# A fused two-block transformer kernel: VectorE's look-ahead in the split norms, two chunks or one

## The reference, cut to what matters

```python
h = rmsnorm(x, norm_mix_g[layer]) * (1.0 + scale_m) + shift_m
mixed = attention_head_groups(h, ...)        # or gated_deltanet, or hybrid_mixer
x = x + gate_m * mixed
h = rmsnorm(x, norm_ffn_g[layer]) * (1.0 + scale_f) + shift_f
x = x + gate_f * swiglu(h, ffn_w_in[layer], ffn_w_out[layer])
```

## Time and profile before

| what | value |
|---|---|
| median of 3 runs | 3710.52 us |
| profiled execution, its own time | 3709.78 us |
| its span, first to last instruction | 3708.1 us |
| mean granted TensorE clock | 0.962 of full |
| TensorE busy | 3413.2 us, 92% of the span |
| TensorE weight loads | 2687.9 us, 72% |
| VectorE busy | 1706.4 us, 46% |
| GpSimd busy | 1387.9 us, 37% |
| ScalarE busy | 1131.3 us, 31% |
| DMA, mean over the span | 95 GB/s |

### The profile page before, as it was taken

The page is one execution under the profiler, slowest core; times in us unless marked ns, Lnnn a source line. Parts: engine busy times, 40 slices in busy tenths (PEclk is TensorE's granted clock), DMA queues, the critical chain, the costliest instruction groups (busy, mean ns, idle before and its releaser), DMA issues. The chain is left out here.

```text
span 3708.1 us, 46261 instructions
## 1 busy us (share of the span) xinstructions
PE 3413.2 (92%) x17788; PEld 2687.9 (72%) x17788; DVE 1706.4 (46%) x3061; ACT 1131.3 (31%) x1422; POOL 1387.9 (37%) x919
## 2 busy tenths in 40 slices
PE   6988999999967779999897998999999998989998
PEld 5864788878667758888695436888899884358887
DVE  5334343437444457474564642744345746521111
ACT  2244322233411132222322343322344322343222
POOL 2323434344553233434231543344410422444434
PEclk9999999999989989999998998999999998999999
DMA  5520344422200014343110001334444320012221
GB/s 227 192 92 9 117 171 152 169 98 91 79 1 1 1 57 170 131 181 142 46 59 33 1 1 57 145 144 170 153 156 173 115 80 1 1 57 84 104 92 62
DMA packets 54653, 353.52 MB, mean 95 GB/s; under 512 B 5856, under 2 KB 6880, under 8 KB 19424
## 3 DMA queue, kind: packets, MB, share of 16 engines
q1 hardware_dynamic: 54208, 349.25, 25.6%
q10 hardware_dynamic: 288, 2.10, 0.1%
HBM read 349.23 MB, written 2.10 MB: 95 GB/s over the span
## 5 line engine op out<-in xcount | busy, mean ns | idle before, releaser
L387 POOL TENSOR_TENSOR W_LO<-ring,W_HI 128x2048 fp32r<-128x2048 f32 (+1 forms) x177 | 729.8, 4123 | 1092.4 <-ACT W_HI L375 1092.4
L443 PE MATMUL PS<-H_HI,W_HI 128*128 128x512 f32 (+1 forms) x1888 | 715.2, 379 | 27.1 <-DVE H_LO L830 21.0
L445 PE MATMUL PS<-H_HI,W_LO 128*128 128x512 f32 (+1 forms) x1888 | 705.2, 374 | 0.0
L444 PE MATMUL PS<-H_LO,W_HI 128*128 128x512 f32 (+1 forms) x1888 | 704.7, 373 | 0.0
L375 ACT ACTIVATE W_HI<-ring 128x2048 fp32r<-128x2048 f32 (+1 forms) x214 | 366.2, 1711 | 481.7 <-PE PS L433 444.6
L443 PEld LDWEIGHTS PS<-H_HI,W_HI 128*128 128x128 f32 x1888 | 360.8, 191 | 91.5 <-issue 31.9
L445 PEld LDWEIGHTS PS<-H_HI,W_LO 128*128 128x128 f32 x1888 | 360.1, 191 | 63.2
L444 PEld LDWEIGHTS PS<-H_LO,W_HI 128*128 128x128 f32 x1888 | 360.9, 191 | 59.7 <-issue 0.2
L872 DVE SCALAR_TENSOR_TENSOR PS<-ring,SC,PS 128x256 f32<-128x256 f32 x768 | 376.2, 490 | 27.0
L431 PE MATMUL PS<-HID_HI,W_HI 128*128 128x512 f32 (+1 forms) x880 | 325.6, 370 | 4.9 <-DVE W_LO L387 4.0
L433 PE MATMUL PS<-HID_HI,W_LO 128*128 128x512 f32 (+1 forms) x880 | 324.0, 368 | 0.0
(11 more groups left out here) (346 smaller groups left out, 5797.2 us busy)
## 6 DMA issues: line engine op xcount, KB each, us to landing
ring<-w_tiles SPq DMA_DIRECT2D x271, 1024.0 KB, 4.8
ring<-d_tiles SPq DMA_DIRECT2D x80, 704.0 KB, 4.1
X<-xT SPq DMA_DIRECT2D x1, 2048.0 KB, 12.4
WORK<-rope_tables ACTq DMA_DIRECT2D x2, 1024.0 KB, 5.5
outT<-H SPq DMA_DIRECT2D x8, 256.0 KB, 2.2
CN<-consts SPq DMA_DIRECT2D x1, 1379.0 KB, 16.3
X<-ctxT SPq DMA_DIRECT2D x1, 1024.0 KB, 9.1
PR<-params SPq DMA_DIRECT2D x1, 465.5 KB, 3.4
```

The source lines that it names most:

```text
L387: eng.tensor_tensor(W_LO[:, b, 0:w], ring[:, g % SLOTS, 0:w], W_HI[:, b, 0:w].bitcast(F32), ALU.subtract).then_inc(sig("tile_split"), 1)
L443: pe.matmul(to, hi[:, cols(k, j)], x_hi(k), start=k == 0, stop=False)
L444: pe.matmul(to, hi[:, cols(k, j)], x_lo(k), start=False, stop=False)
L445: mm = pe.matmul(to, lo[:, cols(k, j)], x_hi(k), start=False, stop=k == n - 1)
```

## The change

In `dve_split_norm` VectorE used to scale two chunks before the first rest and then stay two chunks ahead. Now it scales one chunk first and stays one ahead.

```diff
@@ -813,10 +813,9 @@
         def dve_split_norm(dve, name, gain, shift):
             dve.wait_ge(sig("norm_rstd"), RSTD_NO[name])
             dve_scaled_chunk(dve, NORMED, 0, T, gain, 0)
-            dve_scaled_chunk(dve, NORMED, 0, T, gain, 1)
             for k in range(DC):
-                if k + 2 < DC:
-                    dve_scaled_chunk(dve, NORMED, 0, T, gain, k + 2)
+                if k + 1 < DC:
+                    dve_scaled_chunk(dve, NORMED, 0, T, gain, k + 1)
                 dve_rest_chunk(dve, NORMED, T, shift, k)
```

## The result

The changed kernel takes **3721.77 us** (median of 8 runs, 3719.17 to 3724.34) against 3710.06 for the kernel before (8 runs, 3708.89 to 3713.56). The ratio is 1.0031, 95% interval 1.0023 to 1.0040: slower by 11.7 us, above the predicted range (3712.5 to 3721.0) and in the class to which it gave a chance of 0.34. The profiled execution took 3721.32 us, span 3719.6 us, mean granted clock 0.959 (before 0.962).

The account below looks back on a forecast made before the run. TensorE, busy 92% of the span, was taken as the bound, so time is lost only where it waits. Delays of 3.8 us plus 2.9 for a clock fall in up200, 6.7 over 3709.78, gave 3716.5 us; range 3712.5 to 3721.

Parts of the forecast that it names:

- The sign and the mechanism of the delays: In seven norms, VectorE leaves 0.44 us later and ScalarE's work from A7 on comes 0.87 later, delaying TensorE.
- the waits in front of R0 and R7: On VectorE in each norm: R0 0.21 us late against its slot, R7 another 0.23, both waiting for ScalarE.
- the chain behind A7: ScalarE's rounding, then GpSimd's subtraction to W_LO: 0.87 us later, delaying the second products of up000 and up300 by 0.87 each.
- the lost head start: At up000 and up300 TensorE's first product starts 0.45 us sooner, but this only lengthens the gap before the second.
- the lone early chunk in gdn_in: In gdn_in TensorE starts some 2.8 us sooner with only one chunk; S2 is then held up; net +0.1 us.
- The delays: Later events freeing TensorE, summed over seven norms: 3.8 us, with bounds from 1.7 to 7.1.
- the signal from ScalarE to VectorE: Hand-over time in front of R0 and R7, counted as 0.04 us, the shortest case.
- the bound of 0.22: In each norm, each of VectorE's two new waits could be up to 0.22 us longer than counted.
- up200's fall: Behind up200's gap, growing from 2.60 to about 3.3 us, the clock falls to half for 6.0 us, costing 2.9.
- The gaps of up000 and up300: TensorE's waits before second products grow from 0.84 and 1.15 to about 2.0 and 2.3 us; full clock kept.
- Rival 2: Clock also falls behind up000's or up300's gap: 3718.2 for one, 3719.9 both, 3722.5 both at full price; chance 0.32.
- That execution lies 0.74 under the median: Whole kernel: the profiled 3709.78 us was the forecast's base; its 0.74 difference from the runs' median 3710.52 was not added.

Follow-up runs that it names:

- after again: The changed kernel, unchanged, run and profiled a second time; 3721.72 us, ratio 1.0032 to the kernel before.
- 768 spare columns: The kernel before, plus one unread 128x768 ScalarE activation behind A7 in up000 and up300 only; 3715.67 us, ratio 1.0017.
- only up100 and up200: The kernel before, with the new order only in the norms ahead of up100 and up200; 3712.29 us, ratio 1.0008.
- first rest only: The kernel before, with R0 ahead of S2 in all seven norms, then VectorE back to two chunks ahead; 3713.06 us, ratio 1.0012.
- 768 + 340: The kernel before, plus unread 128x768 and 128x340 ScalarE activations behind A7 in up000 and up300 only; 3714.17 us, ratio 1.0013.
- before again: The kernel before, unchanged, run and profiled a second time; 3708.94 us, ratio 0.9997.
- 280 spare columns: The kernel before, plus one unread 128x280 ScalarE activation behind A7 in up000 and up300 only; 3710.44 us, ratio 1.0002.

## Why the prediction was wrong

- **The sign and the mechanism of the delays: right.** The order, the waits in front of R0 and R7, the lateness handed on by R7 and by the chain behind A7, the lost head start and the lone early chunk in gdn_in all stand in the rows.
- **The delays: right within 0.5 us.** 4.3 against 3.8. The term that was mis-sized is the signal from ScalarE to VectorE: 0.11 in place of 0.04, twice per norm. It lay within the bound of 0.22 that was given. In gdn_in the chain differed too: R0 waited 1.08 us for A0, which stood behind ScalarE's own rounding until 798.77, and got through only with 1.67; the result, 0.13, was as predicted.
- **up200's fall: right.** 2.9 predicted; 2.6 measured behind the gap and 2.4 in the whole stretch, in the two profiles of each kernel.
- **The step that failed**: "The gaps of up000 and up300 grow … below 2.47, so I leave them at full clock." They grew as told (1.87 and 2.21), and the clock fell behind both, 1.61 and 1.56 us. Rival 2 had the place and the price, 1.7 each; that gave 3719.9, 1.9 us under the result. Its 3722.5 is nearer, but by luck: it stands for 3.0 us a fall, which neither cost. What was wrong in the reasoning is the one-sided reading of two rows: 2.47 with a fall and 2.60 without were taken as an edge in the length of the gap, although their order already spoke against one. The runs have falls in front of a second product after 1.86 (after again, up000), 1.87, 1.95, 2.21 and 2.22, and none after 1.86 (768 spare columns, up300), 1.89, 2.10 (only up100 and up200, up300), 2.21 (first rest only, up300), 2.59 and 2.65: the same length on both sides. In front of up200's sums it fell after 2.54 (768 + 340) and not after 2.53 to 2.60 in six other profiles.
- **What no rival had**: falls far from any changed norm, above all 2.5 us between in2 and up200. The forecast with the measured delays and the measured falls at the three gaps would be 3709.78 + 4.3 + 2.4 + 3.2 = 3719.7, inside the range; the 2.5 carry it past. The range took the four places with changed gaps as the only ones at which the clock could change.
- **The reading of the profile.** "That execution lies 0.74 under the median … so I don't add it" did no harm: the medians of before later were 3708.94 to 3710.21.

What stays open is what decides a fall. The gap's length alone does not. Some falls stand in stages that only came a few us sooner or later as a whole, as in the kernel with 768 spare columns; why they come and go there no run shows.

## What to carry to other kernels

Where TensorE is the bound and its clock falls now and then, a change of a few tenths of a us in its gaps can be worth several us (here 4.3 us of delays and 7.8 of clock): put the clock's price, with a chance, on every place where a gap grows, and widen the range for falls elsewhere. To tell such an effect from chance, profile both kernels twice and compare the times from one fixed event to the next; where these recur to a tenth, the difference of two profiles can be trusted stretch by stretch. Look where the profiled execution lies among the runs as well; two here were the slowest of their kernel. Parts that add up in the medians can still differ in every stretch. And a look-ahead of one in a chain through two engines leaves little room for the hand-over: the time of S, A and both signals, here 1.62 us, has to fit into the slots that stand between, here two of 0.66.

## What the hardware showed that was not expected

- Falls of the clock recur: in both executions of the kernel after it was at 0.50 behind the gaps of up000 and up300 and the stretches agree to 0.05 us, though the two executions had reached up000 0.75 us apart.
- The length of a gap does not tell whether it falls: in one execution it fell behind 1.95 us and not behind 2.65. Far from the changed norms, near 1972 us, the kernel before has gaps of 1.99 and then 0.80, the kernel after of 2.05 and 0.80, in front of the same matmuls:

```profile
1972.72 1.13 PE L1557 MATMUL PS<-BIG,CN 128*128 128x512 f32 x2 [1.99 <-DVE BIG L1567]
1974.64 1.13 PE L1557 MATMUL PS<-BIG,CN 128*128 128x512 f32 x2 [0.80 <-DVE BIG L1567]
```

```profile
1976.08 1.13 PE L1556 MATMUL PS<-BIG,CN 128*128 128x512 f32 x2 [2.05 <-DVE BIG L1566]
1978.00 4.00 PE L1556 MATMUL PS<-BIG,CN 128*128 128x512 f32 x4 [0.80 <-DVE BIG L1566]
```

  Two of these matmuls take 1.13 us in the one and four take 4.00 in the other, nearly twice as long for each. At this place the falls do go with the length, by a hair: before again (2.06) and after again (2.30) have one too. So this pair alone does not speak against a rule by length; the gaps at the norms do.
- A one-element activation with another function costs ScalarE a table load of 1.28 us, and the next activation starts 0.01 to 0.02 us behind it, with nothing between (in the kernel with 280 spare columns the load starts at 422.90 and the activation at 424.19; in the kernel after, at 423.16 and 424.46).
